# The head of a one-core residual block: order of the first loads, separate semaphores for three parameter arrays, and the place of the first weight splits

## The reference

```
mod = silu(c) @ w_ada + b_ada
shift, scale, gate = split(mod, 3)
h = rmsnorm(x, norm_pre) * (1.0 + scale) + shift
proj = h @ w_in                     # 6 x 1024 columns
dt = exp(log_dt)                    # per state-space group
mag = exp(min(a_re, -1e-4) * dt);  angle = a_im * dt
```

## Time and profile before

| | us |
|---|---|
| median of 3 runs | 955.14 (954.99 to 955.62) |
| the profiled execution | 955.05 |
| its span, first to last instruction | 953.3 |
| TensorE busy in the span | 930.8 |
| VectorE busy | 640.0 |
| ScalarE busy | 347.7 |

### The profile page before, as it was taken

The page is one execution under the profiler, slowest core; times in us unless marked ns, Lnnn a source line. Parts: engine busy times, 40 slices in busy tenths (PEclk is TensorE's granted clock), DMA queues, the critical chain, the costliest instruction groups (busy, mean ns, idle before and its releaser), DMA issues.

```text
span 953.3 us, 11608 instructions
## 1 busy us (share of the span) xinstructions
PE 930.8 (98%) x4408; PEld 782.3 (82%) x4408; DVE 640.0 (67%) x916; ACT 347.7 (36%) x453; POOL 45.3 (5%) x82
## 2 busy tenths in 40 slices
PE   3999999999999999999999999999999999999997
PEld 3888888888888888888888888888888888888885
DVE  5988899877888887437898789765344444455233
ACT  5741353334444444434444436341022221223111
POOL 0019800000000000000000000000000000000000
PEclk9999999999999999999999999999999999999999
DMA  9743355446555354556898682596543258322222
GB/s 352 298 151 124 124 200 167 155 160 195 173 190 203 142 180 147 191 134 188 220 245 223 136 202 87 166 351 240 183 165 109 89 225 206 143 89 89 89 88 89
DMA packets 95719, 164.60 MB, mean 173 GB/s; under 512 B 38576, under 2 KB 55088, under 8 KB 95664
## 3 DMA queue, kind: packets, MB, share of 16 engines
q1 hardware_dynamic: 85872, 159.31, 51.9%
q10 hardware_dynamic: 9792, 4.56, 1.9%
HBM read 116.64 MB, written 47.19 MB: 172 GB/s over the span
## 4 chain that ended last, share of the span: by engine, by line
PE 96%; DVE 1%; ACT 1%; DMA 1%; issue 0%; ACTq 0%; DVEq 0%
PE ps L1939 49%; PE ps L2059 20%; PE ps L2181 9%; PE psb L2059 8%; PE ps L2130 2%; PE psb L2110 2%; PE psb L2119 1%; PE psa L2098 1%; PE psa L2017 1%; PE psa L1939 1%; DMA par_are<-in_a_re 1%; PE psb L2017 0%; PE psb L1967 0%; ACT gt L1028 0%; DVE mod_out L1400 0%
## 5 line engine op out<-in xcount | busy, mean ns | idle before, releaser
L1939 PE MATMUL ps<-bop,w_hi 128*128 128x512 f32 x1120 | 300.9, 391 | 1.7 <-issue 0.9
L1939 PEld LDWEIGHTS ps<-bop,w_hi 128*128 128x128 f32 x1120 | 209.4, 188 | 44.7 <-issue 2.2
L1939 PE MATMUL ps<-bop,w_lo 128*128 128x512 f32 x560 | 172.6, 390 | 0.0
L1939 PEld LDWEIGHTS ps<-bop,w_lo 128*128 128x128 f32 x560 | 105.2, 188 | 21.9
L1396 DVE TENSOR_TENSOR w_lo<-raw,w_hi 128x1024 fp32r<-128x1024 f32 x43 | 53.2, 1237 | 47.0 <-ACT w_hi L1014 46.8
L2059 PE MATMUL ps<-bop,r_hi 128*128 128x512 f32 x272 | 83.8, 390 | 0.0
L1014 ACT ACTIVATE w_hi<-raw 128x1024 fp32r<-128x1024 f32 x43 | 45.3, 1054 | 71.6 <-PE ps L1939 60.2
L2059 PEld LDWEIGHTS ps<-bop,r_hi 128*128 128x128 f32 x272 | 51.1, 188 | 10.5
L2059 PE MATMUL ps<-t_hi,r_hi 128*128 128x512 f32 x140 | 55.1, 394 | 0.0
L2059 PE MATMUL ps<-t_hi,r_lo 128*128 128x512 f32 x140 | 54.6, 390 | 0.0
L2059 PE MATMUL ps<-t_lo,r_hi 128*128 128x512 f32 x140 | 54.6, 390 | 0.0
(11 more groups left out here) (318 smaller groups left out, 1576.5 us busy)
## 6 DMA issues: line engine op xcount, KB each, us to landing
raw<-in_wstream SPq DMA_DIRECT2D x52, 512.0 KB, 5.2
pair_raw<-in_wstream SPq DMA_DIRECT2D x26, 512.0 KB, 4.3
ada<-in_w_ada SPq DMA_DIRECT2D x16, 512.0 KB, 11.6
x_tok<-in_x SPq DMA_DIRECT2D x8, 512.0 KB, 7.2
gs_d<-gt SPq DMA_DIRECT2D x8, 512.0 KB, 4.9
win_d<-win_new SPq DMA_DIRECT2D x8, 512.0 KB, 2.7
wout_d<-wout_new SPq DMA_DIRECT2D x8, 512.0 KB, 3.8
wout<-wout_d SPq DMA_DIRECT2D x8, 512.0 KB, 4.7
```

What stands on the lines that cost most here:

```text
L1939: last = mm(ps[slot(u)][:, f * HALF:f * HALF + HALF], a[:, k, :], b(k, f), start=k == order[0] and q == 0, stop=k == order[-1] and q == 2)
```

## The change

- The load of cols moves from the head of SP's queue to behind the constants, and both now go behind tile 3 of x; the tiles 0 to 3 lead the queue.
- The three parameter arrays have a semaphore each. a_re is no longer issued by ScalarE at the start but by SP in the middle of w_ada, and is waited for ahead of `magnitudes`.
- The first Sqrt, which loads ScalarE's table, reads log_dt instead of cols; the wait for cols stands ahead of `glub`.
- `exp` for the step sizes is called as soon as log_dt is in; the angles wait for a_im.
- On ScalarE, `xt_out(2)` stands ahead of `split_hi(0)`.
- On VectorE, `split_lo(0)` moves from behind shift_sum(0) to behind scale_sum(1): scale_sum(0), shift_sum(0), scale_sum(1), split_lo(0), split_h(0), shift_sum(1), split_lo(1), scale_sum(2). The rest of the order is as before.

```diff
--- before.py
+++ after.py
@@ -389,7 +389,8 @@
         raw_in, raw_free = two("raw_in"), two("raw_free")
         hi_done, mm_done = sem("hi_done"), sem("mm_done")
         job_out = two("job_out") + [sem("job_out2")]
-        v_sums, par_in, xt_taken = sem("v_sums"), sem("par_in"), sem("xt_taken")
+        v_sums, xt_taken = sem("v_sums"), sem("xt_taken")
+        step_in, aim_in, are_in = sem("step_in"), sem("aim_in"), sem("are_in")
         c_in, silu_ready, mod_ready = sem("c_in"), sem("silu_ready"), sem("mod_ready")
         mod_acc_done = sem("mod_acc_done")
         xt_done, h_hi_done = sem("xt_done"), sem("h_hi_done")
@@ -548,7 +549,6 @@
         def plain_angles(steps):
 
             do, tt, ts = steps.do, nc.vector.tensor_tensor, nc.vector.tensor_scalar
-            exp(steps, par["dt"], par["ldt"], G)
             do(tt(wide["ang"][:, 0:G], par["aim"], par["dt"], ALU.mult))
             do(ts(wide["ang"][:, G:], wide["ang"][:, 0:G], float(CH), None, ALU.mult))
 
@@ -734,11 +734,11 @@
                 sp.wait_ge(job_out[slot(("gs", n))], evicted(("gs", n)))
                 sp.dma_start(gs_d[n], gt[n % 2][:, :]).then_inc(gs_stored[n % 2], 16)
 
-            sp.dma_start(cols[:, :], cols_d).then_inc(cols_in, 16)
             for t in range(CH):
                 sp.dma_start(x_tok[:, t, :], x_view[t]).then_inc(tile_in[t], 16)
-                if t == 2:
+                if t == 3:
                     sp.dma_start(consts[:, :], consts_d).then_inc(small_in, 16)
+                    sp.dma_start(cols[:, :], cols_d).then_inc(cols_in, 16)
             sp.dma_start(silu_row[:, :], c_d).then_inc(c_in, 16)
             for k in range(KT):
                 if k in (1, 2, 3):
@@ -746,6 +746,8 @@
                 for f in range(2):
                     sp.dma_start(ada[:, 2 * (k // 4) + f, :, k % 4, :],
                                  w_ada_d.rearrange("(s k) p m -> k p s m", s=2)[k][:, :, f * HALF:f * HALF + HALF]).then_inc(ada_in[k], 16)
+                if k == 4:
+                    sp.dma_start(par["are"], a_re_d).then_inc(are_in, 16)
             load_w(3)
             sp.wait_ge(h_done, KT)
             for k in range(4):
@@ -1013,12 +1015,11 @@
                     act.wait_ge(mm_done, previous(p) + 1)
                 fn((wx_hi if p == 2 else w_hi[p % 2])[:, :, :], raw[p % 2][:, :, :], ACT.Copy).then_inc(hi_done, 1)
 
-            act.dma_start(par["ldt"], log_dt_d).then_inc(par_in, 16)
-            act.dma_start(par["aim"], a_im_d).then_inc(par_in, 16)
-            act.dma_start(par["are"], a_re_d).then_inc(par_in, 16)
-
-            act.wait_ge(cols_in, 16)
-            fn(stat[:, 5, 0:1], cols[:, 0:1], ACT.Sqrt, scale=0.0)
+            act.dma_start(par["ldt"], log_dt_d).then_inc(step_in, 16)
+            act.dma_start(par["aim"], a_im_d).then_inc(aim_in, 16)
+
+            act.wait_ge(step_in, 16)
+            fn(stat[:, 5, 0:1], par["ldt"][:, 0:1], ACT.Sqrt, scale=0.0)
             done = 0
             for half_, tiles in enumerate(X_TILES_ACT):
                 for t in tiles:
@@ -1032,6 +1033,7 @@
                 fn(stat[:, 2, cols4], stat[:, 1, cols4], ACT.Sqrt).then_inc(x_root, 1)
             act.wait_ge(c_in, 16)
             fn(silu_row[:, :], silu_row[:, :], ACT.Silu).then_inc(silu_ready, 1)
+            act.wait_ge(cols_in, 16)
             fn(glub[:, :], glu_b, ACT.Copy, scale=0.5)
 
             def xt_out(k):
@@ -1056,8 +1058,8 @@
                 act.wait_ge(h_ready, k + 1)
                 fn(hb(0, k), halves(h_full[k][:, :]), ACT.Copy).then_inc(h_hi_done, 1)
 
+            xt_out(2)
             split_hi(0)
-            xt_out(2)
             h_of(0)
             h_high(0)
             xt_out(3)
@@ -1404,7 +1406,9 @@
                 stt(rt[1][:, :], x_tok[:, t, :], 1.0, x_tok[:, t, :], ALU.mult, ALU.mult,
                     accum_out=stat[:, 0, t:t + 1]).then_inc(v_sums, 1)
 
-            dve.wait_ge(par_in, 16 * 3)
+            dve.wait_ge(step_in, 16)
+            exp(steps, par["dt"], par["ldt"], G)
+            dve.wait_ge(aim_in, 16)
             plain_angles(steps)
             for half_ in range(2):
                 cols4 = slice(4 * half_, 4 * half_ + 4)
@@ -1445,12 +1449,13 @@
             for k in range(KT):
                 scale_sum(k)
                 if k == 1:
+                    split_lo(0)
                     split_h(0)
                 shift_sum(k)
                 if k > 1:
                     split_h(k - 1)
-                if k < 2:
-                    split_lo(k)
+                if k == 1:
+                    split_lo(1)
                 if k == 3:
                     split_lo(2)
             split_h(KT - 1)
@@ -1460,6 +1465,7 @@
             cosine(steps)
             cos_sin(steps)
             split_lo(4)
+            dve.wait_ge(are_in, 16)
             magnitudes(steps)
             dve.wait_ge(angle_ready, 1)
             factors(steps)
```

## The result

| | before | after |
|---|---|---|
| median of 22 runs each | 955.15 us (954.58 to 955.71) | 956.43 us (955.00 to 957.23) |
| ratio after / before | | 1.0013, 95% interval 1.0007 to 1.0019 |
| profiled execution, span | 955.05, 953.3 | 956.69, 954.9 |

The change makes the kernel 1.3 us slower, less than the 0.2% that was set as the mark, and inside the range of 954.1 to 957.0. The median lies between the forecast (955.3, give or take 0.4, which it misses) and rival B, the falling clock (956.8), and the spread is twice that of before: 2.2 us against 1.1.

The account below looks back on a forecast made before the run. TensorE never idles from 26.33 us, so only its start can move; w_ada k = 1 bounds it, hiding the 1.05 us gain. 955.05 + 0.2 = 955.25, taken as 955.3, give or take 0.4; range 954.1 to 957.0.

Parts of the forecast that it names:

- rival B: TensorE's clock falls to 1.2 GHz in the longer gap, slowing the first products; 956.8 us, at most 958.5; chance 0.20.
- VectorE is in order, so both now queue behind a landing at 22.8: VectorE's sum for k = 1 and low part wait for w_ada k = 1; first product at 26.5, 0.2 us later.
- The shift of 0.4 us: DMA stream: without cols in front, x and everything behind consts and cols come about 0.4 us earlier, bounds 0 to 0.7.
- The gain of 1.05 us up to Silu: ScalarE: tile 7 squared at 14.7 instead of 15.77, so Silu ends near 18.75 instead of 19.81.
- The gap: TensorE's idle time between transposes and first product: 3.6 us where it was 0.72; 3 to 4 us named as sign.
- The transposes: TensorE's first transposes begin at 11.9 instead of 14.57, take 11.04 us and end at 22.9.
- the point from which it decides an idle time of about 3.2 us: TensorE's clock falls after about 3.2 us without work, read from the fall at the trace's end.
- Bounds 0 to 0.3 us on data that has over 1 us to spare: SP's next load of weights waits for low part 0, at 25.1 instead of 23.7; costs 0 to 0.3 us.
- some 27: SP has DMAs in the queue until some 27 us, so the delayed loads still find the stream busy.
- ScalarE's order: Copy of transposed tile 2 before the split of the weights costs nothing; without cover one copy, about 1.1 us.
- The small load: log_dt lands long before par_are, so VectorE's exponential starts near 2.7 and is over before tile 3 arrives.
- ScalarE's wait: ScalarE's 2.05 us wait for VectorE's statistics, at 13.19 before the change, goes entirely.

Follow-up runs that it names:

- Experiment 1: The changed kernel with VectorE's old order, split_lo(0) again behind shift_sum(0); 954.02 us, ratio to before 0.9989.
- experiment 6: The changed kernel with SP's third load of weights moved behind w_ada k = 3 and the fifth transpose done twice to fill TensorE's gap; 954.90 us.
- experiment 5: The changed kernel with SP's third load of weights moved from ahead of w_ada k = 3 to ahead of k = 4; 956.41 us.
- experiment 2: The changed kernel with the fifth transpose done twice (16 more matmuls), filling TensorE's gap before the first product; 955.55 us.
- experiment 3: The kernel before with only VectorE's new order, split_lo(0) behind the sum for k = 1; 956.49 us.
- 7: The kernel before with VectorE's new order and SP's third load of weights moved behind w_ada k = 3; 955.26 us.
- experiment 10: The changed kernel with VectorE's old order, a_re loaded by ScalarE again and one wait for all three arrays ahead of the exponential; 957.31 us.
- experiment 9: The changed kernel with VectorE's old order and SP's queue as before (cols first, constants behind tile 2 of x); 954.28 us.

## Why the prediction was right, and where not

- **The number.** The forecast itself, 955.3 give or take 0.4, was missed: it said 0.2 us slower, and it is 1.3. The range of 954.1 to 957.0 holds the median because it was drawn out to rival B, which had a chance of 0.20, and a term that no rival had fills up the rest. That the median fell inside is in part luck.
- **The bound.** "VectorE is in order, so both now queue behind a landing at 22.8": right to 0.1 us (22.73, first product 26.41 for 26.5). Experiment 1 (the reordering taken out, 25.31) and experiment 6 (both side effects taken out, 26.16) show the mechanism from both sides. That it is right to 0.1 us is luck of one execution: over the profiled executions w_ada for k = 1 lands between 22.5 and 23.2 with cols ahead (4 kernels, mean 22.8) and between 22.2 and 22.7 with x ahead (9 kernels, mean 22.4). The shift of 0.4 us is right in the mean. The gain of 1.05 us up to Silu was right too (1.19 at Silu's start), and it ended as a wait of VectorE (1.41 us for 1.4).
- **The gap.** Forecast 3.6 us, measured 2.45, outside of the 3 to 4 named as a sign. The transposes began at 12.47 and not at 11.9, and took 11.5 us in place of 11.04, so they ended at 23.96 and not at 22.9. The clock fell all the same.
- **The clock.** The mechanism of rival B was right in place and price (956.8 said; 956.48 with the clock fallen and nothing else wrong), the chance of 0.20 was not: it fell in 12 of 22 executions and in 10 of 11 of experiment 5. The step that failed is "the point from which it decides an idle time of about 3.2 us", taken from the one fall at the end of the trace. Kernels with a profiled gap of 0.5 to 0.7 us never lost it (55 runs, and 93 of before), those with 1.2 to 1.4 us did in 5 of 55, those with 1.6 and 2.45 us in 22 of 33; length alone does not order them, since 1.62 goes with 10 of 11 and 2.45 with 12 of 22. The one fall after 3.2 us idle said nothing of shorter gaps, and the row with 0.72 us and no fall said nothing of longer ones; between the two I should have given it half the chance. The rule that the point moves with a phase of its own (the Trainium skill, TensorE: Matmul & The Clock Gate, Part 1: The HAM clock gate) agrees with this: one and the same kernel keeps the clock in some executions and loses it in others.
- **SP's queue.** "Bounds 0 to 0.3 us on data that has over 1 us to spare" was wrong, and it is the term that was mis-sized. In means, each beside its own runs of before, it costs 0.8 us in the executions of the kernel after that kept the clock (0.83 above before, experiment 6 is 0.05 above), 0.6 in experiment 2 against 6, and 0.8 in experiment 3 against 7. I counted the delay of the issue (25.16 in place of 23.69, 1.5 us) against a backlog of the stream that I had until "some 27", and took it that the stream goes on at its rate once fed. The backlog was gone near 25 (393 GB/s from 24 to 25, 139 from 25 to 26), and the stream came back slowly. Where the clock falls too, this loss is hardly seen (1.49 above before in the kernel after, 1.58 in experiment 5). That a slower TensorE needs w_ada later would explain it, but was not tried.
- **The edits called free.** ScalarE's order: free here, since `w_hi` was done before the sum for k = 1; not in experiment 1, where VectorE waited 0.64 us behind it, nor in experiment 10, where it waited 1.68. The small load: I had the exponential start at 2.7, it starts at 5.15. That did cost something at first: VectorE came to its square of tile 2 only at 9.62, the statistics were late, and 0.91 us of ScalarE's wait stayed where I had none. In experiment 9, with the exponential at 2.74, VectorE waited for ScalarE's squares there and not the other way round. It put the first transposes at 12.47 in place of 11.9, and that vanished in the gap of TensorE.
- **The sum.** 955.3 for a median of 956.43. The 1.1 us between them are the two terms above, the clock in some executions and the queue in others (955.98 where the clock was kept, 956.64 where it fell); with both taken out (experiment 6) the kernel stands at 954.90, level with before.

## What to carry to other kernels

Moving an instruction behind a wait for a transfer moves everything that is queued behind it, and also what other queues wait for from it: follow the semaphores that it raises (here the free buffer, and through SP's in-order queue all of w_ada) before calling it hidden. A step that only lengthens an idle gap of TensorE is not neutral: with gaps of 1.6 and 2.5 us in the profiles, the clock fell in 22 of 33 executions here, which alone cost 1.5 us, and some repeated matmuls in the gap cost nothing that shows and removed it. If a kernel's spread doubles while its median moves little, look for an effect that strikes only a part of the executions, and split them by the granted clock. Kernels that were measured in different groups are compared by their distance to the same kernel in each group: here those groups were 0.15 us apart, as much as some of the differences in question.

## What was not expected of the hardware

The clock fell after TensorE had resumed, more than 1 us into the new work, and stayed at 1.2 GHz for 3.4 us. A DMA stream that had run low (287 GB/s from 26 to 27) came back with 344, then fell to 215 and 227 GB/s with its engines 106 and 94% busy (experiment 3), where the kernel before made 375 and 399 in the same stretches; why is open, it was not tried. The 32 KB load of log_dt from ScalarE's queue, issued at 0.7 us in each case, landed 1.9 us later in the kernel before and 2.0 in experiment 9, where SP's queue begins with the 28 KB of cols, and 4.4 us later in the kernel after and 4.1 in experiment 1, where it begins with tiles of 512 KB.
